# The first expert with its first matrix's blocks held in TensorE and 96 tokens passing, and its second matrix with the 96 tokens held

## The reference, cut to what matters

```
logits = xf @ router_w + router_b ; top_k(4) ; gate = softmax(top_val)
# for each expert e and the tokens sent to it:
hcat  = xf[tok] @ w1[e] + b1[e]                 # 1024 -> 2048
h_glu = minimum(hcat[:, :1024], 7.0)
h_lin = clip(hcat[:, 1024:], -7.0, 7.0)
act   = h_glu * sigmoid(1.702 * h_glu) * (h_lin + 1)
y     = act @ w2[e] + b2[e]                     # 1024 -> 1024
# y of each token = sum over its experts of gate * y
```

## Time and profile before

| what | value |
|---|---|
| median of 3 runs | 2532.51 us (2532.26 to 2533.26) |
| the profiled execution | 2531.16 us, span 2529.4 us |
| PE busy | 2328.4 us (92%) |
| PEld busy | 1588.0 us (63%) |
| DVE, ACT busy | 1098.0 us, 533.8 us |
| mean granted TensorE clock | 0.973 |
| moved by DMA | 608.55 MB |
| HBM read over the span | 240 GB/s |

### The profile page before, as it was taken

The page is one execution under the profiler, slowest core; times in us unless marked ns, Lnnn a source line. Parts: engine busy times, 40 slices in busy tenths (PEclk is TensorE's granted clock), DMA queues, the critical chain, the costliest instruction groups (busy, mean ns, idle before and its releaser), DMA issues.

```text
span 2529.4 us, 34940 instructions
## 1 busy us (share of the span) xinstructions
PE 2328.4 (92%) x14070; PEld 1588.0 (63%) x14070; DVE 1098.0 (43%) x2379; ACT 533.8 (21%) x1307; POOL 59.9 (2%) x78
## 2 busy tenths in 40 slices
PE   6999998899998989979887777999999999999998
PEld 4898865686342423323332224869899898778997
DVE  2555646712111211111111013585875565776863
ACT  3000113511221111111111112452111221432110
POOL 1000000000000000000000000010000000010000
PEclk9999999999999999989999798999999999999999
DMA  8122353156999999899999998323443443223432
GB/s 342 67 100 100 135 215 117 35 218 252 384 419 422 417 421 413 368 421 421 421 421 421 421 421 363 117 84 134 150 140 115 179 150 135 82 84 134 157 119 109
DMA packets 86996, 608.55 MB, mean 241 GB/s; under 512 B 9568, under 2 KB 11744, under 8 KB 16144
## 3 DMA queue, kind: packets, MB, share of 16 engines
q1 hardware_dynamic: 86224, 602.49, 60.1%
q0 software_dynamic: 608, 3.78, 0.4%
HBM read 605.18 MB, written 1.05 MB: 240 GB/s over the span
## 4 chain that ended last, share of the span: by engine, by line
PE 66%; SPq 11%; DMA 9%; PEld 5%; DVE 5%; issue 3%; ACT 2%; PEldq 0%; DVEq 0%; ACTq 0%
PE bank L589 13%; SPq L1083 11%; PE bank L2745 9%; PE bank L711 7%; PE bank L3093 7%; PE bank L621 5%; DMA ring<-in_w_e 4%; PEld bank L589 4%; PE bank L3098 3%; DMA arena<-in_w_e 3%; PE bank L3117 3%; PE bank L691 3%; PE bank L3126 2%; PE bank L3033 1%; PE bank L2831 1%
## 5 line engine op out<-in xcount | busy, mean ns | idle before, releaser
L589 PE MATMUL bank<-arena,ring 128*128 128x272 f32 (+2 forms) x1984 | 455.2, 389 | 5.1 <-DMA ring<-in_w_proj 2.5
L589 PEld LDWEIGHTS bank<-arena,ring 128*128 128x128 f32 x1984 | 376.2, 191 | 72.1 <-DMA ring<-in_w_proj 2.8
L2101 DVE TENSOR_TENSOR arena<-bank,arena 128x256 f32<-128x256 f32 x56 | 23.8, 424 | 772.6 <-PE bank L3066 748.6
L3093 PE MATMUL bank<-arena 128*64 128x512 f32 x616 | 149.6, 613 | 9.2 <-DMA arena<-in_w_e 9.2
L2247 DVE SCALAR_TENSOR_TENSOR arena<-arena,par 128x272 f32<-128x272 f32 (+1 forms) x296 | 148.8, 503 | 10.5
L3098 PE MATMUL bank<-arena 128*32 128x512 f32 x800 | 113.0, 653 | 38.0 <-DMA arena<-in_w_e 37.9
L2745 PE MATMUL bank<-arena 128*128 128x256 f32 (+1 forms) x704 | 130.2, 341 | 0.0
L2745 PEld LDWEIGHTS bank<-arena 128*128 128x128 f32 x704 | 114.5, 191 | 11.6
L711 PE MATMUL bank<-arena 128*128 128x136 f32 (+2 forms) x912 | 105.7, 277 | 0.0
L3093 PE MATMUL bank<-ring,arena 128*64 128x512 f32 x416 | 100.1, 611 | 5.4 <-DMA ring<-in_w_e 5.3
L711 PEld LDWEIGHTS bank<-arena 128*128 128x128 f32 x912 | 104.7, 191 | 0.0
(11 more groups left out here) (514 smaller groups left out, 3334.1 us busy)
## 6 DMA issues: line engine op xcount, KB each, us to landing
arena<-in_w_e SPq DMA_DIRECT2D x207, 1024.0 KB, 25.8
ring<-in_w_e SPq DMA_DIRECT2D x151, 1024.0 KB, 25.3
ring<-in_w_up SPq DMA_DIRECT2D x44, 1024.0 KB, 4.8
ring<-in_w_l SPq DMA_DIRECT2D x37, 1024.0 KB, 4.8
con<-in_w_e SPq DMA_DIRECT2D x26, 1024.0 KB, 26.1
ring<-in_w_ada SPq DMA_DIRECT2D x24, 1024.0 KB, 6.2
ring<-in_w_proj SPq DMA_DIRECT2D x24, 1024.0 KB, 5.8
ring<-in_w_down SPq DMA_DIRECT2D x32, 704.0 KB, 4.1
```

The lines of the kernel that those rows point to most:

```text
L589: mm = pe.matmul(o[:, a:n], ring[:, s, k * 256 + c * P:k * 256 + (c + 1) * P], rhs(k), start=(k == 0), stop=(k == KT - 1))
L3093: mm = pe.matmul(bank[q * PAIR:(q + 1) * PAIR, hidden_bank(g), :], xe[:, (g // CHUNK) % 2, k, s:s + PAIR], w[:, (2 * i + q) * 512:(2 * i + ...
```

## The change

For item 0 alone the first matrix is done the other way round. The 128 rows of unit k are cut into 16 blocks of 128 columns; each block is held in turn and the 96 tokens pass (16 source matmuls for each unit, 32 records). The results lie with features on the partitions, in four banks (4, 5, 2, 3), so nothing is copied or turned: VectorE's activation reads the banks. The second matrix of item 0 holds all 96 tokens at once and passes 512 columns, two source matmuls for each k, into banks 7 and 3; ScalarE copies the results with two instructions. The turning of the first matrix's biases moves from n = 1 to n = 0, behind the last `w1_step(0, 7)` and ahead of the gathers, and so does ScalarE's copy of its result (`b1P`), which now stands ahead of ScalarE's copies of those gathers. The counts of `ht_ready` and `h_turned` fall by three.

```diff
             def turn_b1(k):
-                    mm = pe.matmul(bank[:, 7, k * NE:(k + 1) * NE], b1r[0:NE, k * P:(k + 1) * P], perm[0:NE, 0:NE],
+                    mm = pe.matmul(bank[:, 0, k * NE:(k + 1) * NE], b1r[0:NE, k * P:(k + 1) * P], perm[0:NE, 0:NE],
...
+            def lead_w1(k):
+                w = unit(0, k, True)
+                pe.wait_ge(sem("xe_ready"), lead_part(k) + 1)
+                for c in range(4):
+                    for q in range(4):
+                        at_col = q * 512 + c * P
+                        mm = pe.matmul(bank[:, LEAD_HIDDEN[c], q * LEAD:(q + 1) * LEAD], w[:, at_col:at_col + P],
+                                       xe[:, 0, k, 0:LEAD], start=(k == 0 and q == 0), stop=(k == KT - 1), skip_group_check=True)
+                if k < KT - 1:
+                    mm.then_inc(sem("expert_used"), 1)
+                else:
+                    mm.then_inc(sem("w1_group"), LG)
+
+            def lead_w2():
+                pe.wait_ge(sem("act_ready"), LG)
+                for j in range(4):
+                    w = unit(0, KT + j, True)
+                    for c in range(2):
+                        k = 2 * j + c
+                        for h, b in enumerate(LEAD_OUT):
+                            mm = pe.matmul(bank[0:LEAD, b, :], actL[:, k, :], w[:, c * D + h * 512:c * D + (h + 1) * 512],
+                                           start=(k == 0), stop=(k == KT - 1))
+                    if j < 3:
+                        mm.then_inc(sem("expert_used"), 1)
+                mm.then_inc(sem("w2_item"), 1)
...
-                    if n == 1 and k < 4:
-                        turn_b1(k)
...
                 if n == 0:
+                    pe.wait_ge(sem("bias_loaded"), 32)
+                    for k in range(4):
+                        turn_b1(k)
                     pe.wait_ge(sem("sel_ready"), 2)
                     for b in range(4):
                         gather(0, b, 6 + b % 2)
```

On the other engines:

```diff
             def results(n):
                 act.wait_ge(sem("w2_item"), n + 1)
+                if n == 0:
+                    for h, b in enumerate(LEAD_OUT):
+                        ins = act.activation(ys[0:LEAD, 0, h * 512:(h + 1) * 512], bank[0:LEAD, b, :], ACT.Copy)
+                    ins.then_inc(sem("ys_ready"), LG)
+                    return
...
                 if n == 0:
-                    for g in ITEMS[0][1][:2]:
-                        hidden(g)
+                    act.wait_ge(sem("bias_step"), 1)
+                    act.activation(b1P[:, :, :], bank[:, 0, :].rearrange("p (a b) -> p a b", a=2 * KT), ACT.Copy)\
+                       .then_inc(sem("pgT_ready"), 1)
                     for b in range(4):
                         gathered(0, b, 6 + b % 2)
-                    for g in ITEMS[0][1][2:]:
-                        hidden(g)
...
             def activate(g, n, i):
-                dve.wait_ge(sem("h_turned"), g + 1)
-                wide = paired(n) and i < 2
+                if n == 0:
+                    dve.wait_ge(sem("w1_group"), LG)
+                    raw = [bank[:, b:b + 2, 0:4 * LEAD].rearrange("p c (q t) -> p c q t", q=4)[:, :, :, i * GROUP:(i + 1) * GROUP]
+                           for b in LEAD_HIDDEN[::2]]
+                else:
+                    dve.wait_ge(sem("h_turned"), g + 1 - LG)
+                wide = n > 0 and paired(n) and i < 2
```

More of the change, by code:

```diff
@@ L100, in chunk_due @@
     return found[0] if found else None
-TRIPLE = len(ITEMS[0][1]) > 2
+LG = len(ITEMS[0][1])
+LEAD_HIDDEN = (4, 5, 2, 3)
+LEAD_OUT = (7, 3)
+assert LG == 3 and ITEMS[0][2:] == (True, True) and len(ITEMS[1][1]) == 1
 WIDE_ITEMS = [n for n, item in enumerate(ITEMS) if n > 0 and len(item[1]) == 3]
@@ L120, in hidden_bank @@
         return 7
-    return 3 if TRIPLE and g == 2 else 4 + g % 2
+    return 1 if g == LG else 4 + g % 2
 def third_bank(n):
@@ L921, in program @@
         actT = take(2, KT, 2 * GROUP, at=6656)
+        actL = take(KT, 4 * GROUP, at=6656)[:, :, 0:LEAD]
         sel = take(2, TT, CHUNK * GROUP, at=7680)
@@ L1302, in _ @@
                 for k in range(ka, kb):
-                    ins = act.activation(xe[:, 0, k, 0:LEAD], bank[:, i, (k - ka) * LEAD:(k - ka + 1) * LEAD], ACT.Identity,
+                    ins = act.activation(xe[:, 0, k, 0:LEAD], bank[:, i % 2, (k - ka) * LEAD:(k - ka + 1) * LEAD], ACT.Identity,
                                          bias=mod[:, 24 + k, 0:1])
@@ L1363, in _ @@
                 quad, chunk = quad_due(n), chunk_due(n)
[L1364 to L1367, removed]
                 if n == 2:
@@ L2099, in bias_of @@
                               .to_broadcast([P, 2, 2, PAIR])
-                biased = step(dve.tensor_tensor(by_chunk(gate), by_chunk(bank[:, 6, 0:256]), bias_of(0), ALU.add))
-                linear = step(dve.tensor_tensor(by_chunk(lin), by_chunk(bank[:, 6, 256:512]), bias_of(1), ALU.add))
+                if n > 0:
+                    raw = [by_chunk(bank[:, 6, 0:256]), by_chunk(bank[:, 6, 256:512])]
+                biased = step(dve.tensor_tensor(by_chunk(gate), raw[0], bias_of(0), ALU.add))
+                linear = step(dve.tensor_tensor(by_chunk(lin), raw[1], bias_of(1), ALU.add))
                 dve.wait_ge(sem("moe_step"), biased)
@@ L2111, in activate @@
                 dve.wait_ge(sem("sig_ready"), g + 1)
-                if n >= 2:
-                    dve.wait_ge(sem("w2_item"), n - 1)
+                if n >= 1:
+                    dve.wait_ge(sem("w2_item"), max(n - 1, 1))
                 if i == 2 and n in WIDE_ITEMS:
@@ L2118, in activate @@
                     dst = actT[:, n % 2, 4 * i:4 * i + 4, :]
+                if n == 0:
+                    dst = actL[:, :, i * GROUP:(i + 1) * GROUP]
                 dst = dst.rearrange("p (q c) t -> p c q t", c=2)
@@ L3074, in unit @@
                 return slot(s)
+            def lead_w1(k):
[22 more added lines that the diff above has]
+                mm.then_inc(sem("w2_item"), 1)
             def w1_step(n, k):
+                if n == 0:
+                    lead_w1(k)
+                    return
                 e, groups, first, last = ITEMS[n]
@@ L3082, in w1_step @@
                         pe.wait_ge(sem("ys_ready"), ITEMS[n - 2][1][-1] + 1)
[L3083 to L3087, removed]
+                    elif k == 0 and g >= LG + 2:
+                        pe.wait_ge(sem("ht_ready"), g - 1 - LG)
+                    if k % 2 == 0:
                         pe.wait_ge(sem("xe_ready"), NLEAD + 4 * (g // CHUNK) + k // 2 + 1)
@@ L3105, in w2 @@
             def w2(n):
+                if n == 0:
+                    lead_w2()
+                    return
                 e, groups, first, last = ITEMS[n]
@@ L3156, in _ @@
                         place_routes()
-                    if n == 1 and k < 4:
-                        turn_b1(k)
                     if n == 2:
-                        if k == 6 and TRIPLE:
+                        if k == 6:
                             pe.wait_ge(sem("ys_ready"), 3)
```

22 lines of the change are left out of this document (10 added, 12 removed).

## The result

| | median us | lowest to highest | runs |
|---|---|---|---|
| the changed kernel | 2537.08 | 2534.86 to 2540.13 | 15 |
| the kernel before, beside it | 2530.95 | 2527.99 to 2534.66 | 15 |

The ratio is 1.0024, with a 95% interval of 1.0018 to 1.0031: +6.1 us, where the prediction had +8.9. The kernel before ran 1.6 us faster here than in the three runs of the table further up, and so the absolute time is 4.3 us under the forecast, of which 2.8 us belong to the change. The profiled execution took 2537.95 us; its span is 6.7 us longer than that of the earlier trace rows.

The account below looks back on a forecast made before the run. Expert-weight transfers were taken to bound the layer, through late releases at its head. First matrix +6.2 and biases +3.75 gave release 8 +9.95, height 627.7 against 618.8: +8.9, 2541.4 us; 8 in 10 for 2535.5 to 2545.0.

Parts of the forecast that it names:

- Release 8: Issue of item 1's first weight unit, at 637.68 us before; predicted +9.95 us, to a height of 627.7.
- the second gap: Stretch at 980 to 1060 us where DMA moves 373 GB/s against 420, losing 9.0 us; predicted to stay.
- First matrix: Item 0's first matrix: 113 ns a record, 3.62 us a unit, 0.76 more; +6.2 us in sum.
- Rival (a): First matrix paced by passing columns alone: 83 ns a record, +1.4 us, 2533.9 us; chance 0.07.
- Biases: 32 bias-turning records moved in one run ahead of the gathers: 3.75 us (3.5 to 4.1) more before item 1's first release.
- Gathers: TensorE's gathers behind the biases: unchanged at 5.4 us, ScalarE's added bias copy costing nothing.
- The ruler: Each expert-weight release's height is its time less 2.49 us per unit ahead; the highest line governs while the stream is full.
- release 44: First unit of item 3's second matrix, issued at 728.39 us: height 618.8, taken as governing before the change.
- Second matrix: Item 0's second matrix: starts at 654.3 without waiting for VectorE, takes 14.0 us, +1.4; doesn't count.
- rival (b): Transfers lost at the layer's head don't matter, only TensorE's own delay counts: +3.5 us, 2536.0 us; chance 0.09.
- Rival (c): First matrix's blocks pass faster, 59 ns a record for a 5 us gain: 2527.5 us; chance 0.03.
- (d): First matrix at the 16-column series' pace, 131 ns, or biases bring a new ScalarE wait: 2546.4 us; chance 0.05.

Follow-up runs that it names:

- e2: Changed kernel with item 0's second matrix in its old form (64 and 32 tokens held): 2536.87 us, ratio 1.0023 to the kernel before.
- e3: Kernel before with only the bias turning and ScalarE's copy moved ahead of the gathers: 2534.82 us, ratio 1.0011 to the kernel before.
- e5: Changed kernel with 32 more bias-like records right behind item 0's second matrix: 2536.33 us, ratio 1.0025 to the kernel before.
- e6: Changed kernel with 32 more bias-like records ahead of the gathers: 2543.76 us, ratio 1.0059 to the kernel before.
- e11: Changed kernel with the bias records in four runs of eight, behind units 4 to 7 of item 0: 2535.57 us, ratio 1.0018 to the kernel before.
- e13: Changed kernel with bias records spread over units 4 to 7 and three filler matmuls ahead of the layer: 2533.17 us, ratio 1.0012 to the kernel before.
- e4: Changed kernel with 64 instead of 96 tokens passing in the first matrix, third group's results left out: one execution, 2567.97 us (2530.51 before).
- e9: Kernel before with 32 more bias-like records right behind item 0's second matrix: 2532.85 us, ratio 1.0011 to the kernel before.
- e12: Kernel before with three filler matmuls ahead of the layer and item 0's pair and third group turned every other k: 2528.10 us, ratio 0.9984.
- e10: Kernel before with three filler matmuls at two short waits just ahead of the layer: 2531.69 us, ratio 1.0005 to the kernel before.
- e7: Kernel before with item 0's pair and third group in turned order every other k, for fewer layout changes: 2530.80 us, ratio 1.0002.
- e1: Changed kernel with the bias turning and ScalarE's copy of its result back in n = 1: 2535.65 us, ratio 1.0022 to the kernel before.

## Why the prediction was right, and what was off

**The mechanism held.** Release 8 is TensorE's time through item 0 plus the biases, and the end of the layer follows it. In the changed kernel the last transfer stands 1538.08 - 648.38 = 889.7 us behind release 8. In the other kernels where release 8 is the late one (e2, e3, e5, e6, e11, e13) it is 889.3 to 891.5. Up to the first release of the second gap (1008.01 in the changed kernel, 999.24 before) the distance is 359.4 to 359.7 us in all seven, while release 8 itself ranges over 12.2 us. In the changed kernel work ahead of release 8 counts (e6), work behind it doesn't (e5, e2).

**First matrix.** 614.11 to 621.33 is 64 records at 112.8 ns, predicted 113. Item 0's first matrix took 603.87 to 636.37 = 32.50 us, where before it had taken 26.75: +5.75, predicted +6.2. Rival (a), the passing columns setting the pace, falls with this and with e4's 107 to 110 ns for 64 columns. The Trainium skill, "TensorE: Matmul & The Clock Gate", section "LDWEIGHTS (loading the stationary operand)", gives a load a time by its held columns alone; the estimate of 107 ns from it agrees with e4's 107 to 110, and is 5% under the 112.8 ns with 96 passing.

**Biases.** 3.69 us for a predicted 3.75.

**Gathers.** Predicted unchanged at 5.4; they took 640.06 to 647.11 = 7.05 us, +1.62. This term was wrong, and not by ScalarE's added copy, as I had looked for: the granted clock fell to 0.50 behind the bias run, in the changed kernel and in e3, and didn't in e11.

**Release 8.** 5.75 + 3.69 + 1.62, less 0.37 us for an execution that began the stage earlier, is the +10.7 us of the traces; predicted +9.95. Its height is 648.38 - 19.9 = 628.5, predicted 627.7.

**The reserve under the old line: the mis-sized term.** The prediction took +8.9 us as 627.7 less 618.8, with release 8 of the kernel before 1.0 us under the governing height. The mark of the second gap shows the reserve directly: it moved by 1008.01 - 999.24 = +8.77 us where release 8 moved by +10.70, so the reserve was 1.9 us. e3 shows the same: +2.85 there for +4.77. So 618.8 stood for some 619.7. The ruler assumes that a transfer starts when it is issued. But release 44 of the kernel before, which it took for the governing one, met a queue. Its landing took 6.9 us; in e9, where release 44 was raised by 5.2 us, it took 5.1, and release 8 of the changed kernel, into an empty queue, took 4.8:

```profile
ring<-in_w_e SPq DMA_DIRECT2D x1, 1024.0 KB, 6.9
```

```profile
ring<-in_w_e SPq DMA_DIRECT2D x1, 1024.0 KB, 4.8
```

A transfer that has to queue isn't what the stream waits for, so release 44 didn't govern. e12 against e10 agrees: release 44 came 0.8 us earlier there, release 8 and the last transfer 0.3 us later. What governed instead, 1.9 us above release 8's own line, is open. That the ruler is off by the queue is argued from the landings; no run changed the queue alone.

With release 8 0.75 us later than predicted and the reserve 0.9 us larger, two errors nearly cancelled: +8.77 at that mark for a predicted +8.9. That is luck, and not the precision of the ruler.

**The second gap.** The prediction said that it stays, and its rate did. But the ruler says more than it can there, for the highest line governs only while the stream is full, and here it runs empty: the DMA's rate is 117 GB/s at 1030 to 1040 us (120 at 1040 to 1050 in the changed kernel), and the release of 1043.09, behind it, lands in 4.8 us. From the gap's first release to that one (1050.97 in the changed kernel) TensorE's time counts again:

```profile
999.24:1043.09 43.85, 41.40 (x242) 0.97 0.85 344
1008.01:1050.97 42.96, 40.51 (x242) 1.00 0.84 342
```

It is the same 242 records, and 0.9 us less in the changed kernel. Both kernels idle for 2.45 us shortly ahead of the last release; the eight records that it waits for (from 1040.95 us) ran at half the clock behind that in the kernel before and took 1.71 us, where the changed kernel's (from 1049.71) took 0.88 at the full one. From that release to the last transfer both take 487.0 to 487.1 us. So 0.9 of the predicted 8.9 us went here, and it isn't clear that the change did it: the clock across the gap was full in five of the six other kernels with the new first matrix and in e9, and 0.97 to 0.99 in e3, e6, e7, e10 and e12. The gap also makes part of the spread of 889.3 to 891.5 above.

**Behind the last transfer.** It moved by 1538.08 - 1530.09 = +8.0. The prediction carried +8.9 us through to the end. The second block's first series moved by 1584.02 - 1577.01 = +7.0, so 1.0 of the 8.0 us came back at the hand-over (the kernel before waits 0.70 us within the first series of L3296, the changed one doesn't). The span is 6.7 longer, and the medians say 6.1 (4.6 to 7.8 us by the interval). 8.9 less 0.9 (up to the last transfer), 1.0 (the hand-over) and 0.3 (behind it) is the span's difference.

**Second matrix.** Predicted start 654.3 with no wait for VectorE, and 14.0 us: 654.12, no idle time, and 13.9 (12.6 before). The start is right by luck: the gathers' +1.6 us is made up by item 1's eight units, which took 7.0 us where I had 7.9 (0.88 each, without the biases between them), and by 0.45 in the first matrix and 0.37 in the start. Behind release 8 the second matrix costs nothing, as e2 shows. In the Trainium skill, "TensorEngine Tiling (Array Packing)", section "When to Use Tiling", packing by columns is for 64 held columns or fewer, and the 1.3 us lost with 96 held agree.

**The range and rival (b).** 2537.08 us lies in the range for 8 in 10, but under the 2539 to 2544 that the likeliest account gave, and "slower by more than 5.1 us" holds for the 6.1 though not for all of its interval. Rival (b)'s 2536.0 us is nearer to the measured time than my 2541.4. Its reason is refuted: it has the last transfer stay at 1530 plus 3.5, and the transfer was at 1538.1; it has work behind release 8 count, and e5's didn't; and in e3 the transfer moved by 3.9 us with TensorE's departure only 0.35 later. Rival (c) would have needed 59 ns a record, and (d) 131 ns; neither came.

**The signs named.** Units 3.6 us apart, release 8 at 647 to 648 (648.4), the chain's first transfer at 706.86 instead of behind 781, all came; the last expert transfer came at 1534.88, 8.0 us later, where 1535.8 had been 8.9. The DMA at 600 to 640 us was at 318 GB/s, not 285: only the single transfer of release 8 left that stretch, and the loss fell behind it.

## What to carry to other kernels

In a stage where a stream of transfers is full from some point on, read each release as time less its place in the stream. The highest line sets the end, and TensorE's time counts only ahead of that release. Look at the landings, too: a release whose transfer finds a queue (6.9 us here for 4.8) doesn't govern, and lines read from issues were wrong by 1 us here. Where the stream runs empty again, as at 1037 us, the reading starts anew. Holding blocks of 128 cost a record about 107 to 113 ns with 64, 96 or 129 columns passing (and 131 ns with 16, in a series of another stage), so the turned form of a matmul pays where what it saves (turns, copies) lies ahead of the governing release, and here it lay behind.

## What the chip showed that I had not expected

A TensorE that is never idle can run at the lower clock for a whole stage: with 128 held and 64 passing the granted clock was 0.50 from 600 to 670 us (e4), which is 1.2 GHz; with the same code and 96 passing, the changed kernel, it was 1.00 from 610 on (TensorE alone):

```profile
610.00:640.00 30.00, 30.00 (x267) 1.00 0.85 293
```

Behind one run of 32 records of 32x32 the clock fell to 1.2 GHz, at a loss of about 1.5 us (the changed kernel, e3, e5, e9), and 4.8 us with two such runs (e6). With four runs of eight between units of 96 passing columns it didn't (e11), nor between item 1's units in the kernel before; but in e1, with the same four runs between item 1's units, it did. So spreading such records isn't a sure way to keep the clock. And the half-speed start of expert 0, up to 607 us in the kernel before, was gone with three filler matmuls ahead of it (e10), worth 3.1 us of the stream.
